# The modulation's row sums in a feed-forward group: twelve behind the last tile, or four behind each of the last three

## The reference

```
# first network, each of 2 layers
hf = rms_norm(x, norm_g[2])
ff = square(relu(hf @ w_ff1)) @ w_ff2           # 1024 -> 4096 -> 1024
x  = x + rms_norm(ff, norm_g[3])
...
# second network, each of 2 layers
m_lat = silu(c) @ ada_w[i] + ada_b[i]           # (1024) @ (1024 x 6144)
m_ctx = silu(c_ctx) @ ada_w[i] + ada_b[i]
h_lat = modulate(rms_norm(x_lat, ...), m_lat[:, 0], m_lat[:, 1])
```

## Time and profile before

| | |
|---|---|
| time, median of 3 runs (lowest to highest) | 3916.3 us (3911.31 to 3917.62) |
| the profiled execution's own time | 3916.41 us |
| its span, first to last instruction | 3914.6 us |
| mean granted clock of TensorE | 0.933 |
| PE / DVE / ACT / POOL busy | 90% / 49% / 35% / 15% |
| row sums in the trace (L1264) | 384 weight loads, 384 matmuls, in 16 groups |
| they stand from | 628.5 to 1949.2 us |

### The profile page before, as it was taken

One profiled execution on the slowest core, in us unless ns is written; L12 is line 12 of the kernel. 1 busy time (PEld: TensorE's weight loads), 2 busy tenths in 40 slices (PEclk: granted clock), 3 DMA queues, 4 the chain that ended last, 5 costly groups with the idle time before them and its releaser, 6 DMA issues. The chain is left out here.

```text
span 3914.6 us, 45596 instructions
## 1 busy us (share of the span) xinstructions
PE 3526.4 (90%) x17364; PEld 2858.6 (73%) x17364; DVE 1918.2 (49%) x2408; ACT 1355.6 (35%) x1980; POOL 570.7 (15%) x389
## 2 busy tenths in 40 slices
PE   7887989999788798999967998899999688889998
PEld 5665868887566586888755887788888477767886
DVE  4373337776327333777634651533332444455443
ACT  3265234443326523433323442322122333333222
POOL 0141004333014100433300110100000100010000
PEclk9888989999898899999978999999999899989999
DMA  3101224442210123344210001111111011102221
GB/s 130 67 1 54 97 97 148 152 150 75 87 67 1 43 97 108 134 157 158 78 48 17 18 12 74 44 55 64 64 64 43 33 44 43 43 32 81 96 92 64
DMA packets 58341, 287.09 MB, mean 73 GB/s; under 512 B 9825, under 2 KB 11105, under 8 KB 30945
## 3 DMA queue, kind: packets, MB, share of 16 engines
q1 hardware_dynamic: 58208, 285.34, 20.5%
HBM read 283.21 MB, written 2.10 MB: 73 GB/s over the span
## 5 line engine op out<-in xcount | busy, mean ns | idle before, releaser
L163 PE MATMUL ps<-h_hi,w_hi_rest 128*128 128x512 f32 (+1 forms) x1072 | 390.3, 364 | 38.7 <-DVE w_lo_rest L152 22.5
L1246 POOL TENSOR_TENSOR ada_context<-ada_context,ada_scaled 128x768 f32<-128x768 f32 x112 | 305.8, 2730 | 465.9 <-ACT ada_scaled L1327 461.8
L152 DVE TENSOR_TENSOR w_lo_mix<-w_raw,w_hi_mix 128x2048 fp32r<-128x2048 f32 x96 | 244.7, 2550 | 259.0 <-ACT w_hi_mix L146 258.9
L164 PE MATMUL ps<-h_lo,w_hi_rest 128*128 128x512 f32 (+1 forms) x1072 | 369.8, 360 | 0.0
L163 PE MATMUL ps<-h_hi,w_hi_mix 128*128 128x512 f32 x768 | 313.7, 408 | 17.3 <-DVE w_lo_mix L152 12.7
L166 PE MATMUL ps<-h_hi,w_lo_rest 128*128 128x512 f32 (+1 forms) x1072 | 327.2, 360 | 0.0
L166 PE MATMUL ps<-h_hi,w_lo_mix 128*128 128x512 f32 x768 | 312.0, 406 | 0.0
L164 PE MATMUL ps<-h_lo,w_hi_mix 128*128 128x512 f32 x768 | 311.1, 405 | 0.0
L350 POOL TENSOR_TENSOR x<-x,y 128x512 f32<-128x512 f32 (+1 forms) x32 | 63.8, 1994 | 1604.7 <-DVE y L356 1604.7
L255 PE MATMUL ps<-sq,consts 128*128 128x512 f32 (+1 forms) x372 | 183.3, 643 | 122.8 <-ACT sq L230 122.8
L146 ACT ACTIVATE w_hi_rest<-w_raw 128x2048 fp32r<-128x2048 f32 x82 | 156.3, 1908 | 359.9 <-PE ps L166 357.0
(11 more groups left out here) (385 smaller groups left out, 7808.5 us busy)
## 6 DMA issues: line engine op xcount, KB each, us to landing
w_raw<-in_stream SPq DMA_DIRECT2D x205, 1024.0 KB, 4.8
ada_raw<-in_ada_w SPq DMA_DIRECT2D x128, 384.0 KB, 5.1
cmp_w<-in_cmp_w SPq DMA_DIRECT2D x8, 1024.0 KB, 7.4
mla_raw<-in_stream SPq DMA_DIRECT2D x8, 512.0 KB, 3.6
x<-in_x SPq DMA_DIRECT2D x1, 2048.0 KB, 9.1
out<-x SPq DMA_DIRECT2D x1, 2048.0 KB, 7.3
x<-in_ctx SPq DMA_DIRECT2D x1, 1024.0 KB, 11.3
consts<-in_consts SPq DMA_DIRECT2D x1, 832.0 KB, 11.8
```

Source lines behind the costliest of these rows:

```text
L152: dve.tensor_tensor(k.wlo[:, n % 2, 0:width], k.raw[:, n % 2, 0:width], k.whi[:, n % 2, 0:width].bitcast(F32), ALU.subtract).then_inc(k.w_ ...
L163: pe.matmul(out, whi, xhi, start=start, stop=False)
L164: pe.matmul(out, whi, xlo, start=False, stop=False)
L1246: pool.tensor_tensor(ada.context, ada.context, ada.scaled[:, j % 2, :], ALU.add).then_inc(m["context"], 1)
```

## The change

The 12 sums of a group become three parts of four: one behind tile 9, one behind tile 10, one behind tile 11. The three waits stand ahead of the first part, and the semaphore `summed` is counted up behind the last. The order on the other engines is changed to match. On DVE row 3 comes ahead of the addition of tile 4 to `y` (behind hidden tile 3 and the split of unit n0+3), and rows 4 to 7 behind the additions of tiles 4 to 7. On ACT the scalings 6 and 7 come ahead of the split of unit n0+4. Nothing else is changed; no instruction is added or removed.

```diff
--- before.py
+++ after.py
@@ -1255,15 +1255,17 @@
             unit_ready(pe, k, n0)
             first_tiles(pe, k, n0, 256, 2, tok, lambda i: normed.pe_wait(pe, i), s["ready"])
 
-            def sum_rows(it):
-                pe.wait_ge(m["out"], it)
-                pe.wait_ge(m["latent"], KT * (it + 1))
-                pe.wait_ge(m["context"], (KT - 1) * (it + 1))
-                for c in range(ADA_C):
+            def sum_rows(it, third):
+                if third == 0:
+                    pe.wait_ge(m["out"], it)
+                    pe.wait_ge(m["latent"], KT * (it + 1))
+                    pe.wait_ge(m["context"], (KT - 1) * (it + 1))
+                for c in range(2 * third, 2 * third + 2):
                     for v, part in enumerate((ada.latent, ada.context)):
                         last = pe.matmul(k.ps[:, 3584 + 2 * c + v:3585 + 2 * c + v], part[:, c * P:(c + 1) * P],
                                          k.c["ones"][:, 0:1], start=True, stop=True)
-                last.then_inc(m["summed"], 1)
+                if third == 2:
+                    last.then_inc(m["summed"], 1)
 
             def group(it, first, last_group=False):
                 for j in range(2 if first else 0, T1 + T2):
@@ -1296,8 +1298,8 @@
                     else:
                         last = dense_tile(pe, k, outs, unit_tiles(k, n, 0, 4, 512, (j - T1) % 4), hid_hi, hid_lo, tok)
                     last.then_inc(s["ready"], 1)
-                    if ada and j == T1 + T2 - 1:
-                        sum_rows(it)
+                    if ada and j >= T1 + T2 - 3:
+                        sum_rows(it, j - (T1 + T2 - 3))
 
                     if last_group and y_norm and not ada and j >= T1 + 2:
                         y_norm.pe_add(pe, j - T1 - 2)
@@ -1344,13 +1346,10 @@
                     if ada and j < 3:
                         scale_rows(it, j)
                 if ada:
-                    for j in range(3, 6):
+                    for j in range(3, KT):
                         scale_rows(it, j)
                 if not last_group:
                     split_hi(act, k, n0 + 4, (s["ready"], (T1 + T2) * it + 8), it=it, per=4)
-                if ada:
-                    scale_rows(it, 6)
-                    scale_rows(it, 7)
                 if not last_group:
                     split_hi(act, k, n0 + 5, (s["ready"], (T1 + T2) * it + 12), it=it, per=4)
                 if ada:
@@ -1396,7 +1395,7 @@
                                       ALU.subtract).then_inc(s["hid_lo"], 1)
                     if j % 2:
                         split_lo(dve, k, n0 + j // 2 + 2, it=it, per=4)
-                    if ada and j < 3:
+                    if ada:
                         latent_rows(it, j)
                 for j in range(T2):
                     dve.wait_ge(s["ready"], (T1 + T2) * it + T1 + j + 1)
@@ -1406,8 +1405,8 @@
                         dve.tensor_copy(y[:, j, 0:tok], src).then_inc(s["added"], 1)
                     else:
                         dve.tensor_tensor(y[:, j, 0:tok], src, y[:, j, 0:tok], ALU.add).then_inc(s["added"], 1)
-                    if ada and j < 5:
-                        latent_rows(it, 3 + j)
+                    if ada and j < KT - T1:
+                        latent_rows(it, T1 + j)
                     if j % 4 == 3 and not last_group:
                         split_lo(dve, k, n0 + 4 + j // 4, it=it, per=4)
```

## The result

The changed kernel takes 3930.7 us, median of 7 runs (3927.06 to 3933.72), against 3916.3 us (3911.31 to 3918.2, 7 runs): ratio 1.0036, 95% interval 1.0025 to 1.0047. Another set of runs on another chip gave 1.0034 (1.0024 to 1.0045). So the change costs 10 to 18 us. The forecast was slower by 44 us: the direction holds and the size is off by a factor of three.

A forecast was written before the change was run, and what follows sets the result against it. TensorE's own list of matmuls was taken to bound the kernel. 3916.4 + 33 (wait and sums) + 35 (new slow clock) - 24 (old slow clock) = 3960.4, stated as 3960 us, range 3921 to 3984.

The forecast's parts named there:

- When the rows are ready: DVE and POOL take turns of 2.52 us; row 7 ends at 720.84, so the sums' input is ready 2.85 us earlier.
- What the wait and the sums cost: TensorE waits 2.2 us behind tile 9; per group 4.7 us against 2.6, +2.1 us, in 16 groups +33 us.
- The rest at nothing: ACT's later split, the additions to `y` and SP's loads stay covered; no instruction or DMA added: no cost.
- What the clock costs: Slow clock around the sums: 1.3 stretches a group, 2.2 us, 35 us in 16 groups, in place of 24 us now.
- B: Rival: the wait behind tile 9 is there, but the clock mostly stays up: +9 us, up to +20; chance 0.15.
- C: Rival: rows ready before tile 9 ends, no wait, clock stays up: -25 us, 3891; chance 0.13.

The follow-up runs named there:

- e4: The changed kernel, but POOL adds one column of 768 in each of its additions: 3890.6 us against 3918.3 for the kernel before, ratio 0.9924.
- e5: The kernel before with four more 512-column matmuls, result unused, ahead of tile 11's in each of 16 groups: 3913.7 us against 3916.4, ratio 0.9999.
- e2: The changed kernel's order on ACT and DVE, with all twelve sums back behind tile 11: 3917.9 us against 3918.3 for the kernel before, ratio 0.9998.
- e1: The changed kernel, but six sums behind tile 10 and six behind tile 11, none behind tile 9: 3889.9 us against 3918.3 for the kernel before, ratio 0.9923.
- e7: The changed kernel's order on ACT and DVE, but all twelve sums behind tile 9: 3971.4 us against 3916.4 for the kernel before, ratio 1.0136.
- e6: The kernel before with eight more 512-column matmuls, result unused, ahead of tile 11's in each of 16 groups: 3933.2 us against 3916.4, ratio 1.0043.
- e8: The changed kernel run again unaltered, for a second profile: 3931.3 us against 3919.2 for the kernel before, ratio 1.0034.
- e10: Six sums behind tile 10 and six behind tile 11, ACT and DVE in the order before: 3943.4 us against 3919.2 for the kernel before, ratio 1.0063.
- e9: The changed kernel, but four sums behind tile 10 and eight behind tile 11, none behind tile 9: 3893.1 us against 3919.2 for the kernel before, ratio 0.9937.
- e3: Sums in three parts of four as changed, but ACT and DVE in the order before: 4016.3 us against 3918.3 for the kernel before, ratio 1.0245.

## Why the prediction was off

**When the rows are ready: right.** It had 2.52 us a turn, row 7 ending 2.85 us earlier than before, POOL's last addition 0.8 us ahead of it. The trace has 2.22 us for the wait of 2.2, and 0.81 us between the ends. e4 shows the turns to be the cause. The rule of the Trainium skill that was weighed ("SBUF — State Buffer", "Who interferes with whom") holds in this case as to who waits: 2.0 us beside additions of 768 columns, 1.01 us beside additions of one. It does not hold for the whole recorded length: a turn is 2.52 us, where the shortest addition and the shortest accumulation add up to 1.91 + 1.00 = 2.91.

**What the wait and the sums cost: right.** Forecast +2.1 us a group, 33 us. A group of the changed kernel with no slow stretch lasts 48.47 us, 4.95 more than its 43.52 of tiles. One of the kernel before would last 47.17 - 4 x 0.227 = 46.26 (from e5), 2.74 more. The difference is 2.2 us, 35 us in 16 groups.

**The rest at nothing: right.** e2 is within 0.1%.

**What the clock costs: wrong, and the whole of the miss.** Two terms stood in it. The new pattern was put at 16 x 2.2 = 35 us, 1.3 slow stretches a group. The profile has 8 stretches in 16 groups, 0.5 a group, 12 us. The old pattern was put at 14 x 1.7 = 24 us. It is 28: e1, which has no wait and no fall in the groups, is 26.6 us shorter in the feed-forwards though its sums cost 16 x (2.80 - 2.74) = 1 us more. 22 of these are the 14 groups at 47.83 - 46.26 = 1.57 (the 1.71 of the forecast held 0.14 us that each interruption of the tiles costs, whatever the clock), and the other 6 the norms at the two layers' ends, which the forecast named as evidence and did not count as a gain. So 35 + 12 - 28 = +19, against 33 + 35 - 24 = +44; measured are +19.9 in the feed-forwards and +14.4 in the medians.

The argument that failed is "the gap of 3.0 us is longer than the 2.6 us that now bring one on each time". It took 14 equal groups for 14 independent cases. They are one case, repeated at equal distance; e5 shows that at another distance half of the same gaps go free. The other argument, that the four sums behind tile 10 would prolong a slow stretch, is not borne out in any of the 16 groups. The one long slow stretch is that of the group of 51.59 us, and by the granted clock it ends at 922.4, when the sums behind tile 10 had only begun:

```profile
922.30 0.32 PE L1265 MATMUL ps<-consts,ada_latent 128*128 128x1 f32 x2
```

**The rivals.** The result lies in B (wait, clock mostly up, +9 to +20), which had 0.15, and for B's reason: the wait is whole, and 8 slow stretches stand against 18. C needed a turn of at most 2.1 us; it was 2.52, and e4, where the turns are gone, gives C's time, 28 us below the kernel before. By the Trainium skill's sentence on the clock ("TensorE: Matmul & The Clock Gate", "What's actually happening") activity between the sums keeps the full rate; the trace bears this out in part: none of e4's 46 gaps of 0.81 us inside the layers is caught, and e7 with one gap in place of three is 40 us slower, but 7 of 16 gaps of 2.9 us were still caught.

**Left open.** What decides whether a gap between 2.6 and 3.5 us is caught is shown only so far: not its length alone, and not the group's own work. That it is when the gap comes fits e5, e6 and e8, but no run sets that time by itself. And the medians lie 5 us or so nearer to the kernel before than the profiles' feed-forwards in the changed kernel and in e10. Of this the rest of the program holds 2 to 3 us (3147.6 and 3148.1 in these two profiles, 3150.2 in that of the kernel before); the remainder lies within what one kernel varies between executions.

## What to carry to other kernels

When work is moved to an earlier place on the engine that bounds, compute when its input is ready by the engines that take turns, not by their lone durations; and move it only as far as the input allows. One tile less far (e1) turned +14 us into -28. Small operations in the middle of dense matmuls were cheaper here in pieces than in one block, since the block cost its own time and then the clock's; the second was 28 us of the 72 us that the block cost in all (16 x 2.74 + 28). And a cost that shows at every turn of a regular loop may hang on the loop's period: change the period once before taking it for a rule.

## What the runs showed of the hardware

Adding work made no difference: with 14.5 us more of matmuls e5 takes the time of the kernel before (0.9999), and its profile has 10 slow stretches of 1.56 us in the feed-forwards where the kernel before has 18. With a gap of 2.6 us behind each group, TensorE's clock fell to 1.2 GHz behind 14 of 14 groups of 47.83 us, behind 7 of 14 when the groups had 0.9 us more work, and behind 3 of 14 with 1.8 us more. Gaps up to 1.7 us were not caught inside the layers (46 of 0.8 us in e4, 30 of 1.25 in e1, 14 of 1.7 in e9), gaps of 2.9 us in 7 and 6 of 16, of 3.5 us in 10 of 14, of 4.6 us and more in 16 of 16 (e7) and, near 6 us, in 14 of 14 (e3). Of each gap 0.8 to 2.6 us are one-column sums, in which the profile shows TensorE busy; the fall behind the twelve sums of the kernel before followed 2.6 us of them and no idle time in the profile (724.4 to 726.9: PE busy throughout, at a granted clock of 1.00). Each interruption of the 512-column matmuls by one-column sums also cost about 0.14 us in the tile behind it, beside the gap itself (48.47 - 43.52 - 2.9 - 2 x 0.81 = 0.43 us for three). An accumulation of 128 x 768 numbers on DVE took 1.01 us in all 112 cases when POOL added one column, and 2.0 us in turns with POOL's additions of 768 columns, 2.52 us a turn.
